# One GLA layer in one kernel: the last block's operands for gate and up are made in pairs 1 to 4 from a copy in DRAM, `down` gets two more raw tiles, and the first q products go ahead of the gates

## The reference

```python
hn = rmsnorm(x, norm_mix_g)
q, k, v, r, a_low = split(hn @ w_in)                 # 4 heads, dk 128, dv 256
log_a = log_sigmoid(a_low @ w_a2 + b_a) / 16         # cumulated inside chunks of 64 tokens
...                                                  # chunked attention with a carried state
h = x + (rmsnorm(o) * silu(r)) @ w_out
hn = rmsnorm(h, norm_ffn_g)
h = h + (silu(hn @ w_g) * (hn @ w_u)) @ w_down       # hidden width 2816
out = rmsnorm(h, final_norm_g)
```

## Time and profile before

| | |
|---|---|
| median of 3 runs | 2221.62 us (2219.75 to 2222.63) |
| the profiled execution | 2222.89 us, of which its span is 2221.2 us |
| PE busy | 2152.8 us, 97% of the span |
| PEld, DVE | 1781.8 us (80%), 1358.8 us (61%) |
| ACT, POOL | 821.2 us (37%), 1625.8 us (73%) |
| mean granted clock of PE | 0.992 of full speed |
| DMA | 400.55 MB, mean 180 GB/s |

### The profile page before, as it was taken

One profiled execution on the slowest core, in us unless ns is written; L12 is line 12 of the kernel. 1 busy time (PEld: TensorE's weight loads), 2 busy tenths in 40 slices (PEclk: granted clock), 3 DMA queues, 4 the chain that ended last, 5 costly groups with the idle time before them and its releaser, 6 DMA issues.

```text
span 2221.2 us, 27754 instructions
## 1 busy us (share of the span) xinstructions
PE 2152.8 (97%) x9912; PEld 1781.8 (80%) x9912; DVE 1358.8 (61%) x1778; ACT 821.2 (37%) x1447; POOL 1625.8 (73%) x1294
## 2 busy tenths in 40 slices
PE   7999999999999999879999999999999999999997
PEld 5888888888878888768888877888888878888885
DVE  5346554554555443466667564766757567878786
ACT  4324443344344332344434343443434422142223
POOL 6546675667566756768888886988888886878784
PEclk9999999999999999989999999999999999999999
DMA  5322353335333746763434349443434578669772
GB/s 165 87 77 77 119 189 119 124 118 188 122 124 115 227 125 213 250 209 125 175 130 177 133 166 383 142 171 133 171 142 162 197 287 329 257 235 355 270 315 112
DMA packets 223690, 400.55 MB, mean 180 GB/s; under 512 B 16865, under 2 KB 156129, under 8 KB 214593
## 3 DMA queue, kind: packets, MB, share of 16 engines
q1 hardware_dynamic: 196208, 363.59, 46.1%
q10 hardware_dynamic: 27344, 35.20, 4.7%
HBM read 271.85 MB, written 126.88 MB: 180 GB/s over the span
## 4 chain that ended last, share of the span: by engine, by line
PE 56%; DVE 5%; POOL 4%; issue 2%; DMA 1%; ACT 1%; SPq 0%; ACTq 0%; DVEq 0%; POOLq 0%
PE ps L710 18%; PE ps L712 18%; PE ps L711 18%; POOL w_op L647 2%; DVE acc L1932 1%; POOL ring_lo L638 1%; DMA xop<-x_stage 0%; DVE stage L1456 0%; DMA raw<-in_gla_w_out 0%; POOL w_raw L657 0%; POOL ring_hi L635 0%; POOL w_raw L665 0%; DVE xs L1480 0%; PE ps L845 0%; DVE g L1724 0%
## 5 line engine op out<-in xcount | busy, mean ns | idle before, releaser
L647 POOL TENSOR_TENSOR w_op<-w_raw,w_op 128x512 fp32r<-128x512 f32 x330 | 479.6, 1467 | 113.9 <-ACT w_op L1048 111.1
L710 PE MATMUL ps<-x_op,w_op 128*128 128x512 f32 x1232 | 482.9, 392 | 21.8 <-DVE u L1690 19.8
L711 PE MATMUL ps<-x_op,w_op 128*128 128x512 f32 x1232 | 481.7, 391 | 0.0
L712 PE MATMUL ps<-x_op,w_op 128*128 128x512 f32 x1232 | 481.3, 391 | 0.0
L635 POOL TENSOR_SCALAR ring_hi<-raw 128x512 fp32r<-128x512 f32 x256 | 176.8, 691 | 298.7 <-issue 157.9
L638 POOL TENSOR_TENSOR ring_lo<-raw,ring_hi 128x512 fp32r<-128x512 f32 x256 | 353.5, 1381 | 21.4
L1048 ACT ACTIVATE w_op<-w_raw 128x512 fp32r<-128x512 f32 x330 | 202.3, 625 | 383.4 <-POOL w_raw L665 159.9
L710 PEld LDWEIGHTS ps<-x_op,w_op 128*128 128x128 f32 x1232 | 232.7, 189 | 72.5 <-issue 21.5
L712 PEld LDWEIGHTS ps<-x_op,w_op 128*128 128x128 f32 x1232 | 232.7, 189 | 49.1
L711 PEld LDWEIGHTS ps<-x_op,w_op 128*128 128x128 f32 x1232 | 232.7, 189 | 48.0
L710 PE MATMUL ps<-w_op,hid 128*128 128x512 f32 x616 | 240.8, 391 | 4.3 <-issue 2.1
(11 more groups left out here) (201 smaller groups left out, 3969.7 us busy)
## 6 DMA issues: line engine op xcount, KB each, us to landing
hop<-stage SPq DMA_DIRECT2D x154, 512.0 KB, 2.9
hid<-hop SPq DMA_DIRECT2D x70, 1024.0 KB, 9.4
raw<-in_gla_w_in SPq DMA_DIRECT2D x192, 256.0 KB, 3.3
w_raw<-in_ffn_w_gu SPq DMA_DIRECT2D x176, 256.0 KB, 3.9
w_raw<-in_ffn_w_down SPq DMA_DIRECT2D x88, 256.0 KB, 4.5
xop<-x_stage ACTq DMA_DIRECT2D x42, 512.0 KB, 3.7
x_op<-xop SPq DMA_DIRECT2D x36, 512.0 KB, 8.2
raw<-in_gla_w_out SPq DMA_DIRECT2D x64, 256.0 KB, 3.1
```

Source lines behind the costliest of these rows:

```text
L647: pool.tensor_tensor(shaped(q, tile[:, 1, :]), source(q, i), shaped(q, tile[:, 0, :]).bitcast(F32), ALU.subtract).then_inc(op_ready[i], 1)
L710: pe.matmul(out, l_hi, r_hi, start=first, stop=False, skip_group_check=more)
L711: pe.matmul(out, l_hi, r_lo, start=False, stop=False, skip_group_check=more)
L712: return pe.matmul(out, l_lo, r_hi, start=False, stop=last, skip_group_check=more)
```

## The change

1. **Block 3's operands.** The turned result of block 3 (`xf[1]`, 2 MB) is stored in DRAM (`xlate`) behind the last `x_op` loads, and pair 0 keeps none of the 14 granules and 8 sums. In pairs 1 to 4 one quarter `k` each is read back into `x_in` (512 KB) and worked off as seven high parts (ACT), seven low parts and four sums (DVE) of 128x256 and seven stores of 256 KB issued by ACT, through two tiles `x_late`. The seventh low part and store of a quarter lie in the pair after it. DVE and ACT each get a wait for `xf_stored`; SP gets a load `load_late` in each of four pairs, which from the second on waits for the seventh low part of the quarter before.
2. **Down.** `w_raw_d` gives two more raw tiles for each half, a table `RAW_D` says which tile takes which weights, and loads are placed ahead, one group of them behind a wait for output stores.
3. **Mixer loads.** `load_x` goes behind the second `load_vr`; `load_quad(0)` and `load_quad(1)` go to the ends of the second and third head of block 3.
4. **Start.** PE runs four fp32 matmuls whose result is not used ahead of the first turn and one after the second turn; ACT takes one Sqrt ahead of the first data; `wa_ready` is raised once before and once after the `wa2_parts` step; the first half of the first q product goes ahead of the gates.

```diff
 @sync
-                    if hd == 1 and b == NB - 1:
-                        sp.wait_ge(lc_ready, NB + 1)
-                        load_quad(0)
-                        load_quad(1)
                     load_vr(i + 1, hd, 0)
...
+                    load_vr(i + 2, hd, 1)
                     if hd == H - 1 and 0 < b < NB - 1:
                         wait_operands(b)
                         load_x(b + 1)
-                    load_vr(i + 2, hd, 1)
+                    if hd in (1, 2) and b == NB - 1:
+                        sp.wait_ge(lc_ready, NB + 1)
+                        load_quad(hd - 1)
...
-            for n in range(PER_BLOCK):
-                store_result(NB - 1, n)
+            sp.wait_ge(xf_done, 2 * NT * NB)
+            for kh in range(2):
+                sp.dma_start(xlate[:, :, kh, :].rearrange("k p t -> p k t"), xf[1][kh][:, :, :]).then_inc(xf_stored, 16)
...
                 load_quad(2 * pair + 1)
+                if pair <= 4:
+                    load_late(pair - 1)
...
+            def load_late(k):
+                if k == 0:
+                    sp.wait_ge(xf_stored, 2 * 16)
+                else:
+                    sp.wait_ge(xop_lo, LATE_FROM + len(LATE) * k)
+                sp.dma_start(x_in[:, :, :], xlate[k]).then_inc(x_in_loaded, 16)
...
+        RAW_D = (0, 1, 0, 1, 2, 3, 0, 1, 2, 3, 0, 1, 0, 1, 0, 2, 3, 1, 0, 2, 3, 1)
+        LOADS_AT_ONCE = {6: (12,), 7: (13, 14)}
+        LOADS_AHEAD = {1: (4, 5), 2: (6, 7), 3: (8,), 4: (9, 10), 5: (11,), 8: (17,), 9: (18, 19), 10: (20, 21)}
+        LOADS_AFTER_STORES = {7: (15, 16)}
...
                         store_hid(end, m)
-                        if m in (2, 4):
-                            load_quad(slices[1]["quads"][m // 2 - 1])
+                        if m == 2:
+                            for q in slices[1]["quads"]:
+                                load_quad(q)
 @tensor
+            pe.wait_ge(dve_init, 1)
+            keep_going(4, 6)
             pe.wait_ge(masks, 1)
             for t in range(NT):
                 turn_first(t)
+                if t == 1:
+                    keep_going(1, 6)
             pe.wait_ge(wa_ready, 1)
-            low_rank(0, 0)
+            low_rank(0, 1)
+            column_units(0, 0, ps[:, 0, :], range(KD // 2))
+            pe.wait_ge(wa_ready, 2)
             gates(0, 4)
-            column_units(0, 0, ps[:, 0, :])
+            column_units(0, 0, ps[:, 0, :], range(KD // 2, KD))
 @scalar
+            def late_hi(k, n):
+                i, number = LATE[n], len(LATE) * k + n
+                if i in (4, 5, 0):
+                    act.wait_ge(x_in_loaded, 16 * (k + 1))
+                else:
+                    act.wait_ge(xs_sum, LATE_SUMS + 4 * k + {2: 1, 3: 2, 1: 3, 6: 4}[i])
+                if number >= 2:
+                    act.wait_ge(xop_stored[number % 2], late_stored(number % 2, number // 2))
+                split_hi(x_late[number % 2][:, 0, :], x_late_source(i)).then_inc(xop_hi, 1)
...
                     op_split(q + 1, 4)
                     hidden_hi(pair, 1)
...
+                    if late is not None:
+                        late_hi(late, 4)
+                        late_hi(late, 5)
                     op_split(q + 1, 5)
                     op_split(q + 1, 6)
-                    hidden_hi(pair, 2)
+                    if late is not None:
+                        late_store(late, 4)
+                        late_store(late, 5)
+                    if q != SIDE_BY_SIDE + 1:
+                        hidden_hi(pair, 2)
+                    if late is not None:
+                        late_hi(late, 6)
 @vector
                 if pair == 0:
                     lane_u2(lane)
                     lane_u3(lane)
-                    result_lo(last, 0)
...
                     lane_22(lane, g22)
                     lane_21(lane, g21)
                     lane_12(lane, g12)
                     dve.wait_ge(c12_done, 1)
                     lane_u2(lane + 1)
                     lane_u3(lane + 1)
+                    dve.wait_ge(xf_stored, 2 * 16)
...
                     hidden_lo(pair - 1, 3)
+                    if 2 <= pair <= 5:
+                        late_lo(pair - 2, 6)
                     sum_2(pair - 1)
...
                     lane_12(lane, g12)
+                    if late is not None:
+                        late_lo(late, 0)
+                        late_lo(late, 1)
+                        late_sum(late, 0)
+                        late_sum(late, 1)
                     lane_u2(lane + 1)
                     lane_u3(lane + 1)
+                lane_22(lane + 1, ct)
+                if late is not None:
+                    late_lo(late, 2)
+                    late_lo(late, 3)
+                    late_sum(late, 2)
                 times_gate(pair, g22, 1, c22_done, hid_made)
...
                 hidden_lo(pair, 1)
+                if late is not None:
+                    late_lo(late, 4)
+                    late_lo(late, 5)
+                    late_sum(late, 3)
                 lane_12(lane + 1, ct)
```

More of the change, by code:

```diff
@@ L156, in gla_layer @@
                     [ht[0][th], acc[0][th][0]] for th in range(2)])
+        w_raw_d = [[sb(f"w_raw_d{B}{n}", start, [P, 2048]) for n, start in enumerate(starts)]
+                   for B, starts in enumerate(((OT + 16384, OT + 24576), (XS + 8192, HH + 8192)))]
         xop = nc.dram_tensor("xop", [NS, 7, P, 4, 2, T], F32)
@@ L552, in _ @@
                 B = part["B"]
-                if n > 1:
-                    for q in part["quads"]:
-                        load_quad(q)
+                for number in LOADS_AT_ONCE.get(n, ()):
+                    load_quad(U_QUADS + number)
                 if part["part"] == 0:
@@ L565, in _ @@
                     load_hid(n, i)
+                    if at == 2:
+                        for number in LOADS_AHEAD.get(n, ()):
+                            load_quad(U_QUADS + number)
                     if n > 0 and before["part"] == LAST_SLICE and at == 3:
@@ L712, in three, with column_units @@
                 return pe.matmul(out, l_lo, r_hi, start=False, stop=last, skip_group_check=more)
-            def column_units(i, p, out):
-                for k in range(KD):
+            def column_units(i, p, out, ks=range(KD)):
+                for k in ks:
                     u = 2 * p + k // 4
@@ L876, in bank_free, with keep_going @@
                     pe.wait_ge(c12_done, lane - 1)
+            def keep_going(count, bank):
+                for _ in range(count):
+                    pe.matmul(ps[:, bank, :], scores[:, 0, :], scores[:, :, :].rearrange("p t n -> p (t n)"), start=True,
+                              stop=True)
+            pe.wait_ge(dve_init, 1)
+            keep_going(4, 6)
             pe.wait_ge(masks, 1)
@@ L1198, in _ @@
             act.wait_ge(dve_init, 1)
-            gates(0, 0, 4)
+            gates(0, 1, 4)
             decay_ends(0, 0)
@@ L1321, in _ @@
             turned_result(NB - 1, 3)
-            op_split(1, 1)
-            result_hi(NB - 1, 0)
-            op_split(1, 2)
-            result_hi(NB - 1, 1)
-            result_hi(NB - 1, 2)
-            op_split(1, 3)
+            for i in range(1, 4):
+                op_split(1, i)
             gate_silu(0, 0)
@@ L1343, in _ @@
                     copy_p1(q)
+                late = pair - 1 if 1 <= pair <= 4 else None
                 if q == 1:
-                    op_split(2, 0)
-                    for n in (7, 8, 9):
-                        result_hi(NB - 1, n)
-                    op_split(2, 1)
-                    for n in (10, 11):
-                        result_hi(NB - 1, n)
-                    op_split(2, 2)
-                    for n in (12, 13):
-                        result_hi(NB - 1, n)
-                    op_split(2, 3)
-                elif q == U_QUADS - 1:
+                    act.wait_ge(xf_stored, 2 * 16)
+                if q == U_QUADS - 1:
                     for at, (i, j) in enumerate(made_in(0)):
@@ L1364, in _ @@
                             hidden_hi(pair, 0)
+                        if late is not None and i == 1:
+                            late_hi(late, 2)
+                            late_hi(late, 3)
+                    if late is not None:
+                        late_store(late, 2)
+                        late_store(late, 3)
                 if q == U_QUADS - 1:
@@ L1388, in _ @@
                     gate_silu(pair, 0)
+                    if late is not None:
+                        late_hi(late, 0)
+                        late_hi(late, 1)
                     op_split(q + 1, 4)
@@ L1806, in _ @@
             for pair in range(U_QUADS // 2):
-                last = NB - 1
                 lane = 2 * pair
+                late = pair - 1 if 1 <= pair <= 4 else None
                 if pair == 0:
@@ L1870, in _ @@
                     lane_12(lane, g12)
+                    if late is not None:
+                        late_lo(late, 0)
```

(10 more changed lines are left out.)

143 lines of the change are left out of this document (87 added, 56 removed).

## The result

| | before | after |
|---|---|---|
| median, us (six runs each, taken side by side) | 2221.64 (2215.69 to 2222.63) | 2231.65 (2229.78 to 2234.13) |
| ratio to before, 95% interval | | 1.0051 [1.0038, 1.0064] |
| profiled execution, us (its span) | 2222.89 (2221.2) | 2233.55 (2231.8) |

The forecast was 2213, in a range of 2197 to 2225. The change made the kernel 10.0 us slower.

A forecast was written before the change was run, and what follows sets the result against it. PE, busy 97% of the span, was taken as the bound. Terms -6.1 + 0.6 - 1.4 - 17.4 - 2.6 = -26.9, and +18.0, gave -8.9: 2221.62 to 2213 us, range 2197 to 2225.

The forecast's parts named there:

- The start: Opening up to the first `make_scores`: low-rank product and gates begin earlier, 6.1 us gained, bounds 5.0 and 7.0.
- Mixer loads: Mixer blocks 1 to 3: reordered loads cost +0.6 us in blocks 1 and 2 and gain 1.4 in block 3.
- I take 0.3 us lost in each of the two blocks: Mixer blocks 1 and 2: the `ring_lo` stall moves to `v_lo`, +0.6 us together, bounds -3.2 and +3.
- Pair 0: First gate and up pair: without block 3's operands both u2 waits shrink or go, -17.4 us, bounds -12 and -19.
- no wait near 950: Sign in pair 0: a wait kept near 950 would mean the store of 2 MB was mis-sized.
- the 9.31 us go: Pair 0's second u2 wait: it disappears, as later pairs have no idle before u2, 9.3 us gained.
- `down`: Down projection, second slice: weights loaded together remove the 2.13 us stall, -2.6 us, bounds 0 and -3.
- The other raw tiles answer to no wait of PE in the trace, so I give them nothing: Down projection: the remaining raw tiles loaded ahead bring no gain and no loss, 0 us.
- Pairs 1 to 4: Late work on block 3's operands: 3.7 us PE idle plus 0.8 clock per pair, +18.0 us, bounds 0 and 32.
- 3 x 1.43 = 4.3: Each late pair: the last three DVE operations run beside POOL at 1.43 us each, 4.3 us together.
- The slack of 2.3: Each late pair, from u3 to the next u2: 2.3 us of DVE work may be added without stalling PE.
- the slower rival: Late pairs: SP's `load_late` holds up hidden stores and DVE's even lane, +10 us, 2232 us, chance 0.13.

The follow-up runs named there:

- the start alone: The kernel before with only point 4 of the change, the new opening of PE and ACT: 2215.88 us, 0.9977.
- the loads on ACT: The changed kernel with the loads of the second to fourth quarter of the kept result issued by ACT in place of SP: 2228.32 us, 1.0035.
- 32 columns: The changed kernel with DVE's late operations (28 low parts, 16 sums) on 32 of their 256 columns: 2224.10 us, 1.0010.

## Why the prediction was wrong, step by step

**The start** (-6.1): right, 7.1 measured, a tenth beyond the bound of 7.0; the start alone gave 5.9 in the median. The mechanism held as well: from the gates at 26.92 to the first scores at 46.91 are the 20.0 us of PE's own path. The 6.1 were the middle between a start with a half-clock stretch and one without; this trace has none there.

**Mixer loads** (+0.6 and -1.4): the step that failed is "I take 0.3 us lost in each of the two blocks". The mechanism was right: the stall moves to `v_lo` since the squares wait for `x`. The term was mis-sized. ACT was ready 7.2 us after the first `x` issue, as forecast (7.0). But the four tiles took 9.4 us to land and not 7.3 to 8, of which I had also taken the lower end: the fourth is issued 2.5 us behind the first (1.3 before) and takes 6.9. ACT waited 2.22 us, and 2.36 in block 2. The half-clock stretches of 3.4 and 6.8 us beside the two waits of PE had no term at all; by half of PE's busy time in them they are 1.5 and 2.7. Blocks 1 and 2 cost 4.3 and 4.4 us in place of 0.3 each, together far beyond the upper bound of +3. Block 3 gave back 1.1 of the forecast 1.4.

**Pair 0** (-17.4, measured -18.5): right, with each part: a wait of 1.67 for the forecast 1.6, no wait near 950, no slow stretch. That the 9.31 us go and the 2 MB are stored in time held as well.

**`down`** (-2.6): the second slice's gain was right in its mechanism, the stall of 2.13 is gone, and with 3.5 a little beyond its bound of 3. "The other raw tiles answer to no wait of PE in the trace, so I give them nothing" failed. I looked at what the loads were for and not at what stood behind them in the queue. `ht` was the next load in line, and its lateness cost 4.2 us with the clock. That PE keeps full clock after waits as short as 1.57 and 2.13, as I had read for pair 0, did not hold here: half clock followed the 2.31.

**Pairs 1 to 4** (+18.0): the mechanism, the place and the price of an operation were right, the sum was not. "3 x 1.43 = 4.3" for the last three is 4.27 in the trace. The slack of 2.3 was 1.2 because it was counted from u3, ahead of DVE's last wait for PE, and the first three operations, which I set against it, lie ahead of that wait and cost nothing in pair 1. The two errors nearly cancel: 3.07 in pair 1 for 3.7. That the sum of the four waits with the loads on ACT, 14.6, meets the forecast 4 x 3.7 = 14.8 is therefore luck in part. What was missing is twofold. First, in pairs 2 to 4 of the code SP stood in `load_late` with the hidden stores behind it. I had this as the slower rival's mechanism and gave it 0.13 as a case of its own, in which everything else goes wrong too. It should have been a term of every case: the wait stands in the code, and its price is 4.2 us. Where it shows is the second group of late operations, which runs beside POOL in these three pairs and in only one with the loads on ACT. Secondly, the clock: 8.5 us in four stretches, where I had 0.8 a pair.

The end result stands on the number of the slower rival, 2232. Its mechanism is only a part of the way there: it had 37 us of late cost and no loss elsewhere, and the runs show 27.2 and 12 us of losses in the mixer and `down`. That the two come out alike is chance.

The Trainium skill (SBUF — State Buffer, "The single rule") says that a VectorE operation with two SBUF inputs contends with a GpSimd operation that reads SBUF, and that the order of issue, not the shape, decides who blocks. The runs agree: 32 columns cost 1.27 us beside a POOL operation of 1.3 and 0.19 beside none. The rule tells what DVE pays, not what PE pays: of eleven late operations a pair, three carried 21.5 of the 23.0 us.

**Open.** What brings the second group of late operations beside POOL in some pairs. What decides whether a half-clock stretch follows a wait: with waits of 2.27, 2.57 and 3.07 us none did, with 1.99 and 2.10 one did. How much of the lateness of `ht` is its issue and how much the transfers ahead of it.

## What to carry to other kernels

Work put into an engine's idle time costs its full price, less the slack, behind that engine's last wait for the bottleneck, and ahead of it only what is more than that wait can take up (0.4 us here, which one group used up where it met POOL): find that wait first, then count the slack from there. For every load that is issued earlier, price the load that now stands behind it in the same queue. In this kernel a stall like the four late ones should be booked at about one and a half times its length, because a stretch at half clock mostly comes with it: the four waits of 18.2 us cost 26.7.

## What the hardware showed unexpectedly

A DVE operation of 128x32 with both inputs in SBUF took up to 1.32 us while POOL worked, nearly as much as one of 128x256 (1.50), and 0.18 at its shortest. The length of the stretch at half clock does not follow the wait beside it: 3.4 us with a wait of 2.31 (`down`), 3.4 with 4.53 and 6.8 with 4.31. A wait of 3.07 us in the second late pair of the kernel with the loads on ACT had none behind it.
